# Two transformer blocks on one core: small-block decay levels, diagonal compressed scores, and block 2's attention output formed turned

## The reference, cut to what matters

```python
decay = jnp.exp(jnp.where(causal[:, :, None], rel, -jnp.inf))   # rel = b_t - b_s, per channel
A = jnp.einsum('bhtk,bhsk,bhtsk->bhts', qj, kj, decay)
o = o_inter + jnp.einsum('bhts,bhsv->bhtv', A, vj)
```

```python
s = jnp.einsum('bgrqd,bgnd->bgrqn', qb, k_cmp)          # compressed: 15 keys per group
p_cmp = masked_softmax(s, cmp_end[None, :] <= t_pos[:, None])
o_cmp = jnp.einsum('bgrqn,bgnd->bgrqd', p_cmp, v_cmp)
...
s = jnp.einsum('bgrqd,bgqkd->bgrqk', qr, kg)            # selected blocks
o_sel = jnp.einsum('bgrqk,bgqkd->bgrqd', masked_softmax(s, m_sel), vg)
...
o_win = jnp.einsum('bgrqk,bgkd->bgrqd', masked_softmax(s, m_win), vwb)   # window
out = gt[:, :, 0] * o_cmp + gt[:, :, 1] * o_sel + gt[:, :, 2] * o_win
merged = sigmoid(ga) * (y_a @ w_branch_a) + sigmoid(gb) * (y_b @ w_branch_b)
```

## Time and profile before

| what | value |
|---|---|
| runs shown | median 1287.21 us of 3 (1286.55 to 1287.86) |
| profiled execution | span 1285.2 us; its own device time is not given apart, the median lies 2.0 us above the span |
| TensorE busy | 1116.7 us, 87% |
| VectorE busy | 636.2 us, 49% |
| ScalarE busy | 439.3 us, 34% |
| mean granted TensorE clock | 0.950 |
| block loop, 973.8 to 1014.6 us | TensorE 40.23, VectorE 37.27, ScalarE 33.63 us busy |

### The profile page before, as it was taken

How to read it: one execution, slowest core, us unless ns; L and a number is a source line. 1 busy time by engine, 2 the same in 40 slices (tenths; PEclk the granted TensorE clock), 3 DMA queues, 4 the chain that set the end, 5 groups by cost and what they waited for, 6 DMA issues and landing times.

```text
span 1285.2 us, 16716 instructions
## 1 busy us (share of the span) xinstructions
PE 1116.7 (87%) x7123; PEld 827.3 (64%) x7123; DVE 636.2 (49%) x1031; ACT 439.3 (34%) x624; POOL 9.2 (1%) x19
## 2 busy tenths in 40 slices
PE   7999999897665566656669999999999999999997
PEld 6987898732121122212128988888888889998876
DVE  5998755600000000000006798885767856664466
ACT  4236524110000000000006556553566624454343
POOL 0000000000000000000001000000000000000000
PEclk9999999999788889898879999999979999999999
DMA  8533495699999999999997434453633154455430
GB/s 355 205 145 147 159 366 191 261 429 427 426 427 426 426 427 425 430 425 427 426 425 304 139 121 158 147 169 115 255 134 132 42 185 172 185 197 196 164 131 33
DMA packets 30028, 332.59 MB, mean 259 GB/s; under 512 B 3472, under 2 KB 3744, under 8 KB 5760
## 3 DMA queue, kind: packets, MB, share of 16 engines
q1 hardware_dynamic: 28928, 328.48, 64.5%
q0 software_dynamic: 1024, 3.02, 0.8%
HBM read 330.43 MB, written 1.05 MB: 258 GB/s over the span
## 4 chain that ended last, share of the span: by engine, by line
PE 61%; DMA 29%; DVE 6%; ACT 3%; issue 2%; SPq 0%; DVEq 0%; ACTq 0%
PE ps L609 13%; PE ps L626 11%; PE ps L686 10%; DMA arena<-in_w_down 7%; DMA ring<-in_w_up 7%; DMA arena<-in_w_up 6%; PE ps L1330 6%; DMA ring<-in_w_down 3%; DMA arena<-in_w_gate 3%; PE ps L788 2%; PE ps L967 2%; PE ps L715 2%; PE ps L1141 1%; PE ps L995 1%; PE ps L770 1%
## 5 line engine op out<-in xcount | busy, mean ns | idle before, releaser
L1464 DVE TENSOR_TENSOR parts<-ring,parts 128x2048 fp32r<-128x2048 f32 x70 | 159.9, 2290 | 99.7 <-ACT parts L2285 99.2
L2285 ACT CAST parts<-ring 128x2048 fp32r<-128x2048 f32 x70 | 133.2, 1905 | 154.8 <-PE ps L609 66.7
L626 PE MATMUL ps<-parts 128*128 128x512 f32 x768 | 180.2, 392 | 0.5 <-DVE parts L1464 0.5
L1788 DVE TENSOR_TENSOR arena<-arena,ps 128x512 f32<-128x512 f32 x8 | 5.5, 687 | 341.0 <-PE ps L967 341.0
L609 PE MATMUL ps<-parts 128*128 128x256 f32 x1344 | 163.2, 284 | 0.0
L626 PEld LDWEIGHTS ps<-parts 128*128 128x128 f32 x768 | 142.6, 188 | 31.8 <-issue 2.6
L609 PEld LDWEIGHTS ps<-parts 128*128 128x128 f32 x1344 | 161.9, 192 | 0.2
L686 PE MATMUL ps<-parts 128*128 128x512 f32 x576 | 136.5, 396 | 0.4 <-DVE parts L1633 0.4
L686 PEld LDWEIGHTS ps<-parts 128*128 128x128 f32 x576 | 108.6, 190 | 23.7 <-issue 0.8
L967 PE MATMUL ps<-ring,arena 128*32 128x512 f32 x528 | 76.8, 714 | 45.0 <-DMA ring<-in_w_up 26.3
L967 PE MATMUL ps<-arena 128*32 128x512 f32 x400 | 60.8, 741 | 36.4 <-DMA arena<-in_w_up 19.8
(11 more groups left out here) (367 smaller groups left out, 1402.2 us busy)
## 6 DMA issues: line engine op xcount, KB each, us to landing
ring<-in_units SPq DMA_DIRECT2D x35, 2048.0 KB, 8.4
ring<-in_w_gate SPq DMA_DIRECT2D x19, 2048.0 KB, 43.5
ring<-in_units SPq DMA_DIRECT2D x37, 1024.0 KB, 5.6
ring<-in_w_down SPq DMA_DIRECT2D x15, 2048.0 KB, 44.1
ring<-in_w_up SPq DMA_DIRECT2D x14, 2048.0 KB, 43.2
arena<-in_w_up SPq DMA_DIRECT2D x9, 2048.0 KB, 41.7
arena<-in_w_down SPq DMA_DIRECT2D x9, 2048.0 KB, 45.5
arena<-in_w_gate SPq DMA_DIRECT2D x6, 2048.0 KB, 43.6
```

The costliest lines, as they stand in the source:

```text
L626: mm = nc.tensor.matmul(banks[t], v[:, 4 * h + k, t * P:t * P + P], w[:, k, :], start=h + k + n == 0, stop=h == 1 and k == 3 and n == 2)
L1464: step(V.tensor_tensor(rest_half(name, h), split_half(name, h), w_high[stage][h].bitcast(F32), ALU.subtract), f"{stage}_rest_ready", wait= ...
L2285: step(S.copy(w_high[stage][h], split_half(name, h)), f"{stage}_high_ready", wait=False)
```

## The change

1. *Small blocks.* For levels 0 to 5 only the 32x32 blocks on the diagonal are formed: 64 products per level (8 heads, 2 token tiles, 4 blocks), all in one bank, with block b in partitions 32b to 32b + 31. VectorE drains one bank per level into `scores_block`; after level 5 `place_blocks` copies it in four pieces into `scores_diag`, which has been cleared ahead of the scan. The masks become 32 columns wide.
2. *Diagonal compressed scores.* The keys of two groups lie on the diagonal of `cmp_kT`, so that one product with 128 rows and 30 columns serves an even and an odd head at once: 8 products per token tile into one bank.
3. *Probabilities scaled in place.* `scale_probs` multiplies a block's probabilities by gate over sum on VectorE, and TensorE's transposes (`turn_scaled_probs`) wait for it. The compressed probabilities are scaled by their gate in the same way.
4. *Output formed turned, in one bank.* Values are the stationary side (64 columns), turned probabilities the moving side (512 columns of 4 heads), and the compressed, selected and window parts of a token tile and half add up in one bank that is held (`open_bank(hold=True)`) and skipped by the others. `nsa_out`, y_b and its transposes go; ScalarE and VectorE split the bank directly. The order of blocks becomes token tile, half, branch, and the last block's values stand within branch_b. branch_b's weight rows are permuted ahead.

```diff
@@ TensorE
+                def turn_scaled_probs(blk):
+                    pe.wait_ge(sem("probs_scaled"), blk["n"] - 1)
...
+                def compressed_values(t, half):
+                    o = by_out[t, half] = open_bank(f"y_bT{t}{half}", hold=True)
+                    for i in range(4):
+                        for u in range(2):
+                            g = 2 * half + u
+                            nc.tensor.matmul(o[64 * u:64 * u + 64, i * P:i * P + P], cmp_v[:, g, 64 * i:64 * i + 64], cmp_pT[:, t, g, :],
+                                             start=i == 0, stop=False)
+                def add_values(blk):
...
+                    for j in range(nj):
+                        for u in range(2):
+                            mm = nc.tensor.matmul(o[64 * u:64 * u + 64, :], blk["v"](u, j), probs[:, 4 * u:4 * u + 4, j, :],
+                                                  start=False, stop=blk["branch"] == 1 and j == nj - 1)
+                    if n <= len(IN_BLOCK):
+                        bank = open_bank(f"level{n}")
+                        blocks = bank.rearrange("p (h t q) -> p h t q", h=HG_HEADS, t=TT)
+                        for h in range(HG_HEADS):
+                            for t in range(TT):
+                                for b in range(P // BLOCK):
+                                    own = slice(t * P + BLOCK * b, t * P + BLOCK * b + BLOCK)
+                                    mm = nc.tensor.matmul(blocks[BLOCK * b:BLOCK * b + BLOCK, h, t, :], left[:, h, own], right[:, h, own],
+                                                          start=True, stop=True)
-                    for odd in range(2):
-                        r, g = 64 * odd, 2 * (i // 4) + odd
-                        mm = nc.tensor.matmul(cmp_banks[t][odd][:, i * N_CMP:i * N_CMP + N_CMP], nqT[r:r + 64, i, t * P:t * P + P],
-                                              cmp_kT[r:r + 64, g * N_CMP:g * N_CMP + N_CMP], start=True, stop=True)
+                        mm = nc.tensor.matmul(bank[:, 2 * i * N_CMP:2 * (i + 1) * N_CMP], nqT[:, i, t * P:t * P + P],
+                                              cmp_kT[:, i // 4, :, :], start=True, stop=True)
-                turn_probs(blocks2[0])
...
-                        bank = open_bank(f"cmpO{t}{f}")
+                turn_scaled_probs(blocks2[0])
-                for i in range(3, len(blocks2) + 3):
+                for i in range(3, len(blocks2) + 2):
                     if i < len(blocks2):
                         scores(blocks2[i])
                     if i - 2 < len(blocks2):
-                        turn_probs(blocks2[i - 2])
-                    weigh_values(blocks2[i - 3])
-                    if i == len(blocks2) + 1:
-                        pe.wait_ge(sem("y_b_ready"), 1)
-                        turn_half("y_bT", y_b, 0)
+                        turn_scaled_probs(blocks2[i - 2])
+                    blk = blocks2[i - 3]
+                    if blk["branch"] == 0:
+                        compressed_values(blk["t"], blk["half"])
+                    add_values(blk)
+                split_tokens("branch_b", 0, 0, {})
+                add_values(blocks2[-1])
+                split_tokens("branch_b", 1, 0, {})
@@ VectorE
+                step(V.memset(scores_diag, 0.0), wait=False)
+                        if n == 0:
+                            drain(V.tensor_tensor(dst, bank, wide(mask, [P, HG_HEADS * TT, BLOCK]), ALU.mult), "level0", wait=True)
+                        else:
+                            drain(V.copy_predicated(dst, wide(mask.bitcast(U32), [P, HG_HEADS * TT, BLOCK]), bank), f"level{n}", wait=True)
+                def place_blocks():
+                    diag = scores_diag.rearrange("p (h t q) -> p h t q", h=HG_HEADS, t=TT)
+                    for b in range(P // BLOCK):
+                        own = slice(BLOCK * b, BLOCK * b + BLOCK)
+                        step(V.tensor_copy(diag[own, :, :, own], scores_block[own]), "blocks_placed", wait=False)
+                def scale_probs(blk):
+                    at = 16 * (blk["branch"] + 1) + 8 * blk["half"]
+                    _, _, inv = block_stats(blk)
+                    inverse_sums(blk)
+                    step(V.tensor_tensor(inv, inv, sel_gates[:, blk["t"], at:at + 8], ALU.mult))
+                    step(V.tensor_tensor(blk["p"], blk["p"], wide(inv.unsqueeze(2), [P, HEADS, blk["nk"]]), ALU.mult), "probs_scaled")
-                for i in range(3, len(blocks2) + 3):
+                for i in range(3, len(blocks2) + 2):
+                    if i - 2 < len(blocks2):
+                        scale_probs(blocks2[i - 2])
                     if i < len(blocks2):
                         softmax(blocks2[i])
                     if i - 2 < len(blocks2):
-                        inverse_sums(blocks2[i - 2])
                         probs_turned(blocks2[i - 2])
-                    nsa_out(blocks2[i - 3])
+                    if blk["branch"] == 1:
+                        output_rest_b(blk["t"], blk["half"])
```

More of the change, by code:

```diff
@@ L66 @@
 LEVELS = [1, 2, 4, 8, 16, 32, 64, 128]
+BLOCK = 32
+IN_BLOCK = [L for L in LEVELS if 2 * L <= BLOCK]
 FIRST_SLOTS = [1, 0, 3]
@@ L102, in shape_constants @@
     put("cmp_bias", (seen - 1.0) * np.float32(BIG))
-    for L in LEVELS[:-1]:
-        same = p[:, None] // (2 * L) == p[None, :] // (2 * L)
-        put(f"level{L}", same & (p[:, None] // L % 2 == 0) & (p[None, :] // L % 2 == 1))
+    key, query = p[:, None] % BLOCK, np.arange(BLOCK)[None, :]
+    put("level0", key == query)
+    for L in IN_BLOCK:
+        same = key // (2 * L) == query // (2 * L)
+        put(f"level{L}", same & (key // L % 2 == 0) & (query // L % 2 == 1))
     put("chunk_reset", np.tile(np.arange(T) % CHUNK != 0, (P, 1)))
+    late = sum(x.shape[1] for x in parts) - cols["level0"][0]
+    put("room", np.zeros((P, 3 * T - late)))
     return np.concatenate(parts, 1), cols
@@ L2038, in _ @@
                 bank = filled_by(dve, "cmp_kT")
-                drain(V.tensor_copy(cmp_kT, bank[:, 0:4 * N_CMP]), "cmp_kT")
+                by_pair = bank[:, 0:NSA_KV * N_CMP].rearrange("p (c u n) -> p c u n", c=2, u=2)
+                for u in range(2):
+                    own = slice(64 * u, 64 * u + 64)
+                    ins = V.tensor_copy(cmp_kT[own, :, u, :], by_pair[own, :, u, :])
+                drain(ins, "cmp_kT")
                 for j in range(4):
@@ L2082, in _ @@
+                scale_probs(blocks2[0])
                 softmax(blocks2[2])
-                inverse_sums(blocks2[0])
                 probs_turned(blocks2[0])
-                dve.wait_ge(sem("sel_gates_ready"), 1)
-                for t in range(TT):
-                    for f in range(2):
-                        bank = filled_by(dve, f"cmpO{t}{f}")
-                        g = sel_gates[:, t, 8 * f:8 * f + 8].unsqueeze(2)
-                        drain(V.tensor_tensor(grid(y_b[:, t, f * 512:f * 512 + 512], HEADS), grid(bank, HEADS), wide(g, [P, HEADS, 64]), ALU.mult),
-                              f"cmpO{t}{f}", wait=True)
@@ L2094, in nsa_out @@
-                def nsa_out(blk):
-                    t, half_, branch = blk["t"], blk["half"], blk["branch"]
-                    _, _, inv = block_stats(blk)
-                    at = 16 * (branch + 1) + 8 * half_
-                    step(V.tensor_tensor(inv, inv, sel_gates[:, t, at:at + 8], ALU.mult))
-                    bank = filled_by(dve, f"{blk['name']}O")
-                    tmp_ = page(9, 1024, 512)
-                    drain(V.tensor_tensor(grid(tmp_, HEADS), grid(bank, HEADS), wide(inv.unsqueeze(2), [P, HEADS, HEAD_DIM]), ALU.mult),
-                          f"{blk['name']}O", wait=True)
-                    y = y_b[:, t, half_ * 512:half_ * 512 + 512]
-                    step(V.tensor_tensor(y, y, tmp_, ALU.add), "y_b_ready" if branch and half_ else "dve_step")
```

187 lines of the change are left out of this document (106 added, 81 removed).

## The result

| | median us | lowest to highest | runs |
|---|---|---|---|
| before | 1287.53 | 1286.55 to 1290.19 | 4 |
| changed | 1298.95 | 1296.28 to 1300.40 | 4 |

The ratio is 1.0082, with a 95% interval of 1.0070 to 1.0095: the changed kernel is slower by 0.8%, 11.4 us of the medians. The sign was forecast, the size was not: 1290.2 us was predicted, and the measured time lies 0.95 us above the range's upper end of 1298.0.

The account below looks back on a forecast made before the run. TensorE was taken as busy nearly throughout, with VectorE nearly level and deciding what is won. -7.5 levels, 0 compressed scores, +8.0 block loop and +2.5 clock give +3.0 on 1285.2, plus 2.0: 1290.2 us, range 1284 to 1298.

Parts of the forecast that it names:

- Levels: Levels up to the second attention's start: shorter small-block levels, limited by VectorE, make that start 7.5 us earlier.
- the 0.3: Level 1: clearing scores_diag delays VectorE's chain by about 1.8 us, so the projection starts only 0.3 us earlier.
- Compressed scores: Compressed scores: 16 products of 128x30 replace 32 of 64x15, with no gain while the granted clock falls.
- Block loop at full clock: Block loop to branch_b: VectorE's scaling delays TensorE's transposes and the work queued behind; 8.0 us slower.
- The clock: Block loop: half clock behind TensorE's two long new idles costs 2.5 us, bounds 0 and 7.
- The two idles that had a price: TensorE's idles of 4.9 us ahead of block 0's transposes and 6.3 ahead of block 7's: 2.5 us for both.
- VectorE's slack of 1.8 us at the end of branch_a: Block loop: this slack hides part of the clock loss, 1.8 us, behind the idle ahead of block 0's transposes.
- The other waits: Waits behind levels 0 and 4 and block-loop idles of 1.4 to 3.1 us, given no clock cost.
- No loss of clock: New block-loop idles bring no half clock, or it falls where VectorE is awaited anyway: 1287.7 us; chance 0.22.
- The clock stays up at the compressed scores: Compressed scores: the 3.37 us idle brings no half clock, winning 5.1 us: 1282.6 to 1285.1 us; chance 0.16.
- Small products are bound by their number: Levels: each takes 3.2 us, so the gain shrinks from 7.5 to 1.2: 1296.5 us; chance 0.12.
- Value products don't pair: Block loop: each pair of 512-column value products takes 1.7 us, some 8 us more: 1298 us; chance 0.03.

Follow-up runs that it names:

- e8: Kernel before plus small-block levels and diagonal compressed scores, with idle TensorE products at levels 0, 1, 4 and in the 3.4 us wait; 1279.65 us, ratio 0.9940.
- e3: Changed kernel plus idle TensorE products ahead of the waits behind levels 0, 1, 4 and ahead of transposes of blocks 0, 1, 5, 6, 7; 1291.67 us.
- e4: Changed kernel with the in-place probability scaling cut to 8 columns per head, so output isn't the reference's; 1289.09 us, ratio 1.0004 to before.
- e5: Changed kernel with the scalings of blocks 0 and 1 moved earlier in VectorE's order, no work removed; 1289.62 us, ratio 1.0012 to before.
- e6: Changed kernel with the scalings of blocks 0, 1 and 7 moved earlier in VectorE's order; 1282.27 us, ratio 0.9955 to before.
- e1: Kernel before with only the small-block levels added; 1284.05 us, ratio 0.9963 to before.
- e2: Kernel before with small-block levels and diagonal compressed scores, block loop as before; 1281.90 us, ratio 0.9956 to before.
- e7: e6 plus idle TensorE products at levels 0, 1, 4, ahead of blocks 4 to 6 and in the 3.4 us wait; 1276.98 us, ratio 0.9913 to before.

## Why the prediction was off

- **Levels, forecast -7.5: measured -4.7.** Level 1 gave nothing for the 0.3: VectorE's chain behind the scan sets it, at 763.39. At full clock (e8) the levels take 6.3 us less than before, so 1.2 of the 7.5 were layout. Most of that, 1.0, is at levels 2, 3 and 5: in e8 they give 2.1 us each for some 2.5, since a level takes 1.23 us for 1.1 and was 3.5 before for 3.6. The four copies behind level 5 (1.77 us together for 2.2) cost 0.65 for 1.0. The other 1.6 are the half clock behind level 4. The slow projection behind level 0 costs nothing, since TensorE waits for VectorE behind level 1 anyway.
- **Compressed scores, forecast 0: right.** The same wait of 3.37 us stayed and the same half clock with it: 7.04 us for 7.01.
- **Block loop at full clock, forecast +8.0: right.** The waits came within 0.2 us of the layout where they were priced, and e3 corrected for its one slow place has 67.5 us for 67.0. e4, e5 and e6 move it as the order of VectorE's work says.
- **The clock, forecast +2.5: this step failed, in two ways.** Differences of starts between the changed kernel and e3, where the clock stayed up at these places, tell what each stretch cost.
- *The two idles that had a price cost 4.2 us for 2.5.* From block 0's to block 1's transposes the changed kernel takes 16.71 us and e3 14.36, which is 2.35 for the first idle; from block 7's transposes to branch_b it takes 6.50 for 4.64, which is 1.86 for the last. "VectorE's slack of 1.8 us at the end of branch_a hides a part" was wrong: block 1's scaling stands on VectorE behind the drain of branch_a's second half, and this drain waits for TensorE, so the late product makes everything late.
```profile
972.38 0.69 DVE L2116 TENSOR_TENSOR ring<-ring,ps 128x512 f32<-128x512 f32 x1 [3.30 <-PE ps L707]
...
973.41 1.22 DVE L2157 TENSOR_TENSOR arena<-arena,small 128x1024 f32<-128x1024 f32 x1
```
- *The other waits had no price and cost 2.4.* The prediction has idles of "1.4 to 3.1 in between" and waits behind levels 0 and 4, and puts nothing on them; its only word on short idles is that those "of 1 to 2 us in the trace brought none". Four waits of 1.88 to 2.73 us brought a stretch each. The one behind level 4 cost 1.6 us (levels column, 125.22 for 123.62 in e8). The one for y_b's bank made the scores 1.67 us longer, of which 0.8 came through (25.22 us from block 1's to block 5's transposes, 24.38 in e3): VectorE had to wait for these scores, but only for a part of that.
```profile
985.69 0.42 DVE L1497 CUSTOM_DVE_ANT_0 ring<-ps,consts 128x256 f32<-128x256 f32 x1 [0.77 <-PE ps L759]
```
- Behind level 0 and ahead of block 5 the stretch cost nothing, since TensorE waits for VectorE soon after: level 1's projection starts 22.12 us after level 0 with it and without it (e8), and block 6's transposes 7.04 us after block 5's in both traces.
- **The sum again.** 4.2 + 1.6 + 0.8 = 6.6 in place of 2.5, and -6.3 for the levels at full clock, give -6.3 + 0 + 8.0 + 6.6 = 8.3, against 10.6 of the spans. Of the rest 0.5 lies in the block loop (67.5 for 67.0), 0.2 in the compressed stage, 0.4 in branch_b (1.2 for 0.8), 0.5 is the wait for cmp_v's weights, which was to stay at 0.43 and is 0.97, and 0.7 is elsewhere, within what single runs differ by. The 7.7 us that e3's runs gave back are no second proof of the 6.6: the levels and blocks columns of its profiled execution gave 4.0, with two places still at half clock (1.0 and 1.6 us), and its runs go from 1288.64 to 1293.38.
- **Rivals.** *No loss of clock* fell: six stretches. *The clock stays up at the compressed scores* did not happen, but its 3.7 us for the scores was right (3.76 in e8). *Small products are bound by their number* fell: 128 records in 1.30 us, 10 ns each. The 25 ns floor that the Trainium skill, "TensorE: Matmul & The Clock Gate" (on small matmuls), gives from start to start does not hold for products that go to four column groups in turn. *Value products don't pair* fell.

What stays open is why a wait of 2.2 to 2.5 us brings the half clock in one run and not in another: behind level 0 it did in the changed kernel, e4 and e5 (12.51 to 12.79 us), and not in e1, e2 and e6 (11.13 to 11.14). Nor is a wait of this length needed: in e7 and e8 the clock fell at and behind the compressed scores, with no wait above 0.41 us ahead.

## What to carry to other kernels

When two engines are nearly level, work taken off one is only worth what the other can follow: write down the second engine's order and put first what the first engine waits for, above all multiplications that have moved ahead of a dependent. The same edit cost 0.8% in the order as written, and gained 0.45% with three scalings moved. Price every new wait of TensorE with the clock that may go behind it, not only the longest (here 1.88 us was enough), and ask of each whether the next engine's work hides it: of six stretches, two cost nothing and one cost half. Fill the waits with idle products if their cause must stay, and look at the trace again, for the clock can fall elsewhere.

## What the hardware showed unexpectedly

- 32x32 float32 products in four column groups: 128 records in 1.30 us (10 ns each), against 64 in 1.21 us in two groups.
- Half clock behind waits of 1.88, 2.18, 2.55 and 2.73 us, each with 1.4 to 1.7 us more on the next instructions, though waits of 1.03 and 1.26 in the same trace brought none. Behind the 3.37 us it lasted longer: 3.3 us more on the scores (7.04 for 3.76) and 2.2 on the projection (13.33 for 11.16).
- Idle products keep the clock up at some places and not at others: in e3 and e7 the half clock began in level 1 itself (1.48 and 1.66 us for 1.30) and covered the seven idle products behind it (1.68 and 1.67 us, 0.94 in e8).
